# Two-layer conformer and latent-attention trunk: one stop of TensorE per unit of gate weights, four heads at four stages

## What is computed

```python
proj   = rms(x) @ w_in[l]                 # convolution input, latents, and 4 x 512 gate columns
u      = silu(layer_norm(depthwise_conv31(a * sigmoid(gate)) + conv_b))
y_conv = u @ w_conv_out[l]                # 512 -> 1024
q, k   = rope(rms(...)), rope(rms(...))   # per head, 96 wide
p      = softmax(mask(q @ k.T * scale))   # blocks of 128 queries; block 0 sees 128 keys, block 1 all 256
o      = p @ v                            # per head, 64 wide
y_mla  = o @ w_mla_out[l]                 # 512 -> 1024
gates  = sigmoid(proj[..., o4:] + gate_bias)
x      = x + (gates[0] * y_conv + gates[1] * y_mla) @ w_out[l]
```

## Time and profile before

| | |
|---|---|
| median of 3 runs | 1056.39 us |
| the profiled execution | 1056.12 us |
| its span, first to last instruction | 1054.3 us |
| outside the span | 1.8 us |
| TensorE busy | 1047.7 us (99% of the span) |
| VectorE busy | 677.6 us (64%) |
| ScalarE busy | 578.2 us (55%) |
| granted TensorE clock | 1.00 on the mean |

### The profile page before, as it was taken

One profiled execution on the slowest core, in us unless ns is written; L12 is line 12 of the kernel. 1 busy time (PEld: TensorE's weight loads), 2 busy tenths in 40 slices (PEclk: granted clock), 3 DMA queues, 4 the chain that ended last, 5 costly groups with the idle time before them and its releaser, 6 DMA issues.

```text
span 1054.3 us, 13846 instructions
## 1 busy us (share of the span) xinstructions
PE 1047.7 (99%) x5057; PEld 875.6 (83%) x5057; DVE 677.6 (64%) x897; ACT 578.2 (55%) x778; POOL 245.6 (23%) x258
## 2 busy tenths in 40 slices
PE   9999999999999999999999999999999999999998
PEld 6888888998888888888888888889978888888887
DVE  6755654698976666555476555646999667656551
ACT  7654544576872665445276454536778537545440
POOL 2960000148850000000048400001588300000000
PEclk9999999999999999999999999999999999999999
DMA  9977666455655396676469767655366356885641
GB/s 285 309 242 220 186 206 197 136 184 175 204 168 162 104 324 182 208 229 198 130 181 288 213 213 222 185 172 167 129 207 224 115 160 182 272 234 180 208 140 40
DMA packets 176771, 205.14 MB, mean 195 GB/s; under 512 B 49328, under 2 KB 147920, under 8 KB 176720
## 3 DMA queue, kind: packets, MB, share of 16 engines
q1 hardware_dynamic: 175504, 202.35, 61.4%
q10 hardware_dynamic: 1216, 2.11, 1.0%
HBM read 192.90 MB, written 1.05 MB: 184 GB/s over the span
## 4 chain that ended last, share of the span: by engine, by line
PE 88%; DVE 7%; DMA 2%; ACT 1%; issue 1%; SPq 0%; POOL 0%; ACTq 0%; DVEq 0%
PE bank L618 27%; PE bank L616 27%; PE bank L617 27%; DVE wlo L1433 2%; DVE bank L1601 2%; DMA raw<-in_w_in 1%; PE bank L697 1%; PE bank L655 1%; PE bank L892 1%; DVE small L1660 1%; PE bank L870 1%; PE bank L861 1%; DMA x<-in_x 1%; ACT whi L1076 0%; PE bank L894 0%
## 5 line engine op out<-in xcount | busy, mean ns | idle before, releaser
L1433 DVE TENSOR_TENSOR wlo<-raw,whi 128x2048 fp32r<-128x2048 f32 (+2 forms) x152 | 347.3, 2289 | 88.2 <-ACT whi L1076 87.1
L616 PE MATMUL bank<-whi,hThi 128*128 128x512 f32 (+1 forms) x976 | 378.9, 388 | 0.0
L618 PE MATMUL bank<-whi,hTlo 128*128 128x512 f32 (+1 forms) x976 | 373.7, 383 | 0.0
L617 PE MATMUL bank<-wlo,hThi 128*128 128x512 f32 (+1 forms) x976 | 373.5, 383 | 0.0
L1076 ACT ACTIVATE whi<-raw 128x2048 fp32r<-128x2048 f32 (+2 forms) x176 | 335.3, 1910 | 27.7 <-DMA raw<-in_ffn_w_up 17.2
L618 PEld LDWEIGHTS bank<-whi,hTlo 128*128 128x128 f32 x976 | 183.2, 188 | 35.9
L616 PEld LDWEIGHTS bank<-whi,hThi 128*128 128x128 f32 x976 | 183.3, 188 | 35.2 <-issue 0.6
L617 PEld LDWEIGHTS bank<-wlo,hThi 128*128 128x128 f32 x976 | 183.4, 188 | 34.8
L1145 ACT ACTIVATE gates<-bank,small 128x256 f32<-128x256 f32 x88 | 41.8, 475 | 275.6 <-PE bank L618 275.0
L616 PE MATMUL bank<-whi,gThi 128*128 128x512 f32 (+1 forms) x416 | 162.4, 390 | 0.0
L618 PE MATMUL bank<-whi,gTlo 128*128 128x512 f32 (+1 forms) x416 | 161.2, 387 | 0.0
(11 more groups left out here) (162 smaller groups left out, 819.6 us busy)
## 6 DMA issues: line engine op xcount, KB each, us to landing
raw<-in_ffn_w_down SPq DMA_DIRECT2D x88, 512.0 KB, 4.2
raw<-in_ffn_w_gate SPq DMA_DIRECT2D x84, 512.0 KB, 4.5
raw<-in_ffn_w_up SPq DMA_DIRECT2D x84, 512.0 KB, 5.6
raw<-in_w_in SPq DMA_DIRECT2D x48, 512.0 KB, 4.9
raw<-in_w_out SPq DMA_DIRECT2D x16, 512.0 KB, 4.3
raw<-in_w_in SPq DMA_DIRECT2D x8, 544.0 KB, 4.5
raw<-in_w_mla_out SPq DMA_DIRECT2D x8, 512.0 KB, 4.0
raw<-in_w_conv_out SPq DMA_DIRECT2D x8, 512.0 KB, 4.8
```

Source lines behind the costliest of these rows:

```text
L616: nc.tensor.matmul(out, lh, rh, start=start, stop=False, skip_group_check=skip)
L617: nc.tensor.matmul(out, lh, rl, start=False, stop=False, skip_group_check=skip)
L618: return nc.tensor.matmul(out, ll, rh, start=False, stop=stop, skip_group_check=skip)
L1433: nc.vector.tensor_tensor(wlo[:, slot(u0, RING), 0:n], raw[:, slot(u0, RAW), 0:n], whi[:, slot(u0, RING), 0:n].bitcast(F32), ALU.subtract) ...
```

## The change

The products of a gate unit stop once, at the unit's end, for four steps of four heads: `head_values(u8-2)`, `head_probs(u8-1)`, `head_scores(u8)`, `head_turn(u8+1)`. In the last unit `head_values(5)` stands ahead of t = 1 and `head_probs(6)` with `head_scores(7)` in the middle of t = 1, behind a wait for `ot_lo` of head 5. At the unit's end come `conv_turn`, `head_values(6)` and `head_probs(7)`; `head_values(7)` stands in the middle of the attention's output projection of t = 0, ahead of its unit i = 1, with waits for `ot_lo` of the heads 4 to 7. `head_probs` uses bank 6, `head_values` the last quarters of the banks 5 and 6, in three products of 128 columns with always 128 columns of stationary data, `conv_turn(1)` bank 4. The lists of ScalarE and VectorE are rewritten to match. On VectorE `head_rest(6)` and `head_rest(7)` both stand ahead of `bn_aggr`.

```diff
             def head_values(l, h):
                 pe.wait_ge(pt_ready, l * H + h + 1)
+                pe.wait_ge(max_ready, l * (2 * H) + min(2 * h + 4, 2 * H))
                 if h:
                     pe.wait_ge(ot_lo, l * H + h)
                 p = pT[:, h % 2, :]
-                n = (h % 2 + 1) * VD
-                v = vtok[:, :, h - h % 2:h + 1, :].rearrange("p t h d -> p t (h d)")
-                nc.tensor.matmul(bank[0:n, 6, 0:2 * P], v[:, 0, :], p[:, 0:2 * P], start=True, stop=False,
-                                 skip_group_check=True)
-                nc.tensor.matmul(bank[0:n, 6, P:2 * P], v[:, 1, :], p[:, 2 * P:3 * P], start=False, stop=True,
-                                 skip_group_check=True).then_inc(pv_done, 1)
+                v = vtok[:, :, h - h % 2:h - h % 2 + 2, :].rearrange("p t h d -> p t (h d)")
+                nc.tensor.matmul(bank[:, 5, 3 * P:4 * P], v[:, 0, :], p[:, 0:P], start=True, stop=True)
+                nc.tensor.matmul(bank[:, 6, 3 * P:4 * P], v[:, 0, :], p[:, P:2 * P], start=True, stop=False)
+                nc.tensor.matmul(bank[:, 6, 3 * P:4 * P], v[:, 1, :], p[:, 2 * P:3 * P], start=False,
+                                 stop=True).then_inc(pv_done, 1)
...
                     for t in range(TT):
-                        if u8 == 0 and t == 1:
+                        if (u8, t) == (0, 1):
                             head_turn(l, 0)
+                        if (u8, t) == (H - 1, 1):
+                            head_values(l, H - 3)
...
                         for k in range(4):
                             if (u8, t, k) == (H - 1, 1, 2):
-                                head_values(l, H - 2)
+
+                                pe.wait_ge(ot_lo, l * H + H - 2)
+                                head_probs(l, H - 2)
+                                head_scores(l, H - 1)
...
-                        if t == 0 and u8:
+                    if u8 < H - 1:
+
+                        if u8 > 1:
+                            head_values(l, u8 - 2)
+                        if u8:
                             head_probs(l, u8 - 1)
-                            head_scores(l, u8)
-                        if t == 1:
-                            if u8 == 0:
-                                head_scores(l, 0)
-                            elif u8 < H - 1:
-                                head_values(l, u8 - 1)
-
-                head_probs(l, H - 1)
+                        head_scores(l, u8)
+                        head_turn(l, u8 + 1)
+
                 for t in range(TT):
                     conv_turn(l, t)
-                head_values(l, H - 1)
-
-                def out_half(h):
-
-                    pe.wait_ge(ot_lo, l * H + 4 * h + 4)
+                head_values(l, H - 2)
+                head_probs(l, H - 1)
...
+                def last_values():
+
+                    head_values(l, H - 1)
+                    outputs(H - 2)
 
                 for t in range(TT):
                     pe.wait_ge(gate_sum, l * 8 + (6 if t == 0 else 8))
                     rows_out(l, UM + M_MLA, 2, gT, t, 2 - 2 * t, mla_done,
-                             between={0: lambda: out_half(0), 1: lambda: out_half(1)} if t == 0 else
+                             between={0: lambda: outputs(4), 2: last_values, 3: lambda: outputs(H)} if t == 0 else
                              {0: lambda: ln_turn(l)})
```

The list of VectorE (that of before is in the code above):

```diff
+                taps(8)
+                for h in range(H - 2):
+                    head_max(h)
+                    taps(3)
+                    head_sum(h)
+                    if h > 1:
+                        head_rest(h - 2)
+                    if h % 2:
+                        gate_bias(h // 2)
+                    taps(10)
+                head_max(H - 2)
+                taps(1)
+                head_rest(H - 4)
+                taps(2)
+                head_sum(H - 2)
+                taps(2)
+                head_rest(H - 3)
                 taps(4)
...
+                head_max(H - 1)
+                taps(3)
+                head_sum(H - 1)
                 taps(CT * W)
...
-                head_rest(H - 1)
+                for h in (H - 2, H - 1):
+                    head_rest(h)
                 for t in range(TT):
                     dve.wait_ge(ln_stats, l * TT + t + 1)
```

The list of ScalarE:

```diff
                 head_copy(0)
...
+                for h in range(H - 1):
+                    if h:
+                        head_probs(h - 1)
+                    head_copy(h + 1)
+                    if h == H - 2:
+
+                        act.wait_ge(max_ready, l * (2 * H) + 2 * h + 2)
+                        head_hi(h - 2)
+                        head_exp(h)
+                        head_scale(h)
+                        head_hi(h - 1)
                         one()
+                    else:
+                        head_exp(h)
+                        if h > 1:
+                            head_hi(h - 2)
+                        one()
+                        head_scale(h)
+                    if h % 2:
+                        gate_tanh(h // 2)
+                    elif h in (2, 4):
+                        one()
+                head_probs(H - 2)
+                head_exp(H - 1)
+                head_scale(H - 1)
                 head_probs(H - 1)
+                head_hi(H - 2)
                 head_hi(H - 1)
                 gate_tanh(3)
```

More of the change, by code:

```diff
@@ L905, in rows_out @@
                     for k in range(2):
+                        if 2 * i + k in between:
+                            between[2 * i + k]()
                         for m in range(2):
@@ L1045, in mixer @@
                 rows_out(l, UM + M_CO, 2, hT, 0, 4, co_done,
-                         between={0: lambda: conv_half(0), 1: lambda: conv_half(1)})
-                rows_out(l, UM + M_CO, 2, hT, 1, 6, co_done, between={1: lambda: y_turn(0)})
+                         between={0: lambda: conv_half(0), 2: lambda: conv_half(1)})
+                rows_out(l, UM + M_CO, 2, hT, 1, 6, co_done, between={2: lambda: y_turn(0)})
                 pe.wait_ge(yt_lo, l * 4 + 2)
-                rows_out(l, UM + M_WO, 4, hT, 0, 4, acc_done, between={3: lambda: y_turn(1)})
+                rows_out(l, UM + M_WO, 4, hT, 0, 4, acc_done, between={6: lambda: y_turn(1)})
                 pe.wait_ge(yt_lo, l * 4 + 4)
-                rows_out(l, UM + M_WO, 4, hT, 1, 2, acc_done, between={3: lambda: norm(l, 2, 0)})
+                rows_out(l, UM + M_WO, 4, hT, 1, 2, acc_done, between={6: lambda: norm(l, 2, 0)})
             pe.sem_inc(unit_free, RING)
@@ L1338, in head_hi @@
                     rows = slice(h % 2 * VD, (h % 2 + 1) * VD)
-                    nc.scalar.activation(gThi[rows, h // 2, :], bank[rows, 6, 0:SEQ], ACT.Copy).then_inc(ot_hi, 1)
+                    nc.scalar.activation(gThi[rows, h // 2, :].rearrange("p (t n) -> p t n", t=TT),
+                                         bank[rows, 5:7, 3 * P:4 * P], ACT.Copy).then_inc(ot_hi, 1)
                 def gate_tanh(g):
@@ L1354, in mixer @@
                 head_copy(0)
-                for u8 in range(1, 8):
-                    if u8 == 1:
-                        head_exp(0)
-                        head_scale(0)
-                    head_copy(u8)
-                    if u8 > 1:
-                        head_hi(u8 - 2)
-                    one()
-                    head_probs(u8 - 1)
-                    if u8 % 2 == 0:
-                        gate_tanh(u8 // 2 - 1)
-                    head_exp(u8)
-                    if u8 in (3, 5):
-                        one()
-                    if u8 == H - 1:
-                        head_hi(u8 - 1)
-                    head_scale(u8)
+                for h in range(H - 1):
[8 more added lines that the diff above has]
+                        head_hi(h - 1)
+                        one()
+                    else:
[11 more added lines that the diff above has]
+                head_scale(H - 1)
                 head_probs(H - 1)
+                head_hi(H - 2)
                 head_hi(H - 1)
@@ L1701, in head_rest @@
                     rows = slice(h % 2 * VD, (h % 2 + 1) * VD)
-                    rest(gTlo[rows, h // 2, :], bank[rows, 6, 0:SEQ], gThi[rows, h // 2, :]).then_inc(ot_lo, 1)
+                    rest(gTlo[rows, h // 2, :].rearrange("p (t n) -> p t n", t=TT), bank[rows, 5:7, 3 * P:4 * P],
+                         gThi[rows, h // 2, :].rearrange("p (t n) -> p t n", t=TT)).then_inc(ot_lo, 1)
                 def gate_bias(g):
@@ L1712, in gate_bias @@
                                                 bias[:, :], ALU.add).then_inc(gate_sum, 1)
-                taps(4)
-                head_max(0)
-                taps(2)
-                head_sum(0)
-                for u8 in range(1, 8):
-                    taps(4)
-                    if u8 > 1:
-                        head_rest(u8 - 2)
-                    taps(3)
-                    if u8 % 2 == 0:
-                        gate_bias(u8 // 2 - 1)
-                    head_max(u8)
```

(11 more changed lines are left out.)

21 lines of the change are left out of this document (9 added, 12 removed).

## The result

The changed kernel takes 1063.00 us (median of 6 runs, 1062.61 to 1064.74), the one before 1056.09 (6 runs, 1055.77 to 1056.65). The ratio is 1.0066, 95% interval 1.0055 to 1.0077: slower by 6.9 us. The forecast was 1060.6, with a range of 1057.4 to 1063.5.

The account below looks back on a forecast made before the run. TensorE, busy 1047.7 of 1054.3 us, was taken as the bound. Per layer -0.70 - 1.12 - 0.20 + 2.5 + 1.6 = +2.1 us, +4.2 for two layers: 1056.39 + 4.2 = 1060.6 us, range 1057.4 to 1063.5.

Parts of the forecast that it names:

- wait of `head_probs(0)`: Gate phase: TensorE's wait for head 0's scaled probabilities becomes hidden behind 24 products, -0.70 us a layer.
- narrow `head_values`: Even heads' 64-column operation becomes 128 columns, saving 0.28 us at each of four heads, -1.12 us a layer.
- five stops: Gate phase and projection: 12 stops instead of 17, at 0.04 us each, -0.20 us a layer.
- stall before `conv_turn`: First tail, end of the last unit: TensorE waits for VectorE's last taps, +2.5 us a layer (2.3 to 2.9).
- stall before `ln_turn`: Second tail, in the output projection: TensorE waits for the layer norm, +1.6 us a layer (1.4 to 1.9).
- clock: Rival: TensorE's clock falls to 1.2 GHz behind the stalls, adding 8.2 us, 1068.8; chance 0.05.
- The forecast's own bounds: Whole kernel: the terms' extremes give +1.6 to +3.1 us a layer, 1059.6 to 1062.6.
- The prediction's bound of 2.9: Upper end of the stall before `conv_turn`, if ScalarE's rounding ahead of `head_probs(6)` pushes `head_exp(7)`.
- The tails are hidden: Rival: VectorE's taps and layer norm keep ahead of TensorE, only -2.0 us a layer stands, 1052.4; chance 0.07.
- only the first tail is real: Rival: values to layer norm take under 2.8 us instead of 4.4, +0.5 a layer, 1057.4; chance 0.10.
- VectorE paces the middle: Rival: TensorE waits for probabilities up to 0.5 us in three units a layer, +3, 1063.5; chance 0.10.
- first rival: Tails hidden, kernel faster: decides when both stalls together stay under 1.5 us a layer; 1052.4, chance 0.07.

Follow-up runs that it names:

- experiment 4: Changed kernel with `head_rest(7)` behind `gate_bias(3)` instead of ahead of `bn_aggr`: 1059.24 us, ratio 1.0023.
- experiment 5: Changed kernel with four taps moved earlier into VectorE's idle time, none left behind `head_sum(7)`: 1058.36 us, ratio 1.0019.
- experiment 3: Kernel before with `head_probs(0)` six products later and, on ScalarE, `head_copy(1)` ahead of `head_exp(0)` and `head_scale(0)`: 1054.62 us, ratio 0.9986.
- experiment 1: Kernel before with `head_values` always on 128 columns of stationary data: 1054.11 us, ratio 0.9979.
- experiment 6: Changed kernel with ten bf16 matmuls of zeros put into the stall before `conv_turn`: 1061.62 us, ratio 1.0050.
- experiment 2: Kernel before with only `head_probs(0)` moved six products later, to a stop of its own: 1056.25 us, ratio 0.9999.
- experiments 8 and 9: Kernel before, two stops a unit kept: 8 with the edits of experiment 1 and experiment 2, 1055.27 us; 9 with those of experiment 1 and experiment 3, 1053.97 us.
- experiment 7: Changed kernel with the four taps ahead of `head_max(7)` moved behind it, lengthening the stall before `conv_turn`: 1068.29 us, ratio 1.0111.
- experiment 11: Changed kernel with both tails mended (1052.51 us) given a second stop again in units 2 to 6, for `head_values(u8-2)`: 1054.26 us.

## Why the prediction was right, and where it was short

**The sign and the place** were right. Both stalls are where the lists of the engines put them, and the experiments 4 and 5 took the second away (1.68 us a layer) and the first by as much as four taps are long (1.61 us a layer), as expected.

**Term by term, per layer.**

| term | predicted | measured |
|---|---|---|
| wait of `head_probs(0)` | -0.70 | -0.71 (experiment 3) |
| narrow `head_values` | -1.12 | -1.02 (experiment 1) |
| five stops | -0.20 | -0.10, an estimate at 0.02 each (units of 7.57 against 7.55) |
| stall before `conv_turn` | +2.5 | +2.76 |
| stall before `ln_turn` | +1.6 | +1.65 |
| sum | +2.1 | +2.55 (layer 0), +2.52 (both layers of experiment 6) |
| clock | 0 | +1.6 in layer 1 |

The measured terms sum to +2.58. For two layers +5.1 came from the stalls and gains where +4.2 was forecast, +1.6 from the clock, and +0.3 lies ahead of the changed stretch, within the spread of that part.

**The range** held by luck. The forecast's own bounds, +1.6 to +3.1 a layer, gave 1059.6 to 1062.6, or 3.2 to 6.2 us over the kernel before; measured were 1063.0 and 6.9. The stated range reached to 1063.5 only because it was widened for another rival, VectorE as the pace of the middle, which did not happen. What filled that room was the clock, for which the sum had nothing.

**The first stall** was 0.26 longer. The prediction let head 7's maximum start 0.05 behind the scores. VectorE's timeline of the changed kernel:

```profile
294.45 0.43 DVE L1454 TENSOR_TENSOR gTlo<-bank,gThi 64x256 fp32r<-64x256 f32 x1 [0.50 <-ACT gThi L1345]
294.91 1.67 DVE L1617 SCALAR_TENSOR_TENSOR bank<-cu,vec,bank 128x256 f32<-128x256 f32 x4
296.62 0.35 DVE L1704 CUSTOM_DVE_ANT_0 htok<-bank,mask,small 128x128 f32<-128x128 f32 x1
...
298.47 0.16 DVE L1713 RECIPROCAL small<-small 128x2 f32<-128x2 f32 x1
298.55 0.86 DVE L1617 SCALAR_TENSOR_TENSOR bank<-cu,vec,bank 128x256 f32<-128x256 f32 x2
299.31 0.88 DVE L1609 TENSOR_SCALAR cacc<-bank,vec 128x256 f32<-128x256 f32 x2
```

The scores' record ends at 296.26, the maximum starts at 296.62: VectorE had waited 0.50 for head 5's high part and had four taps to do first. From the maximum on the chain has the length predicted (3.57 us to the last tap). The prediction's bound of 2.9 allowed for this size, but for a delay on ScalarE. The term was mis-sized by the state of the engine that starts it.

**The wait that went** was rightly sized and wrongly explained. The prediction named the scaled probabilities, by the earlier trace rows, the row of the weight load. They were ready at 247.91, in time; late was ScalarE's copy of head 1 (experiment 2). The sum came out by luck: the change moves that copy ahead as well as the probabilities back.

**The narrow operation and the stop.** The 0.28 was 0.255 and the 0.04 was 0.02. The title of the change, one stop of TensorE a unit, is the smallest of its terms: 0.1 us a layer.

**The step that failed is the clock.** It stood as a rival with 0.05, on the ground that the clock had been 1.00 through the phase. That trace had no idle time over 0.5 us there, and so it said nothing about a stall of 2.8. The mechanism of this rival was right, its chance was too small and its price too high. It took as much loss as the stalls are long, 8.2 us; measured is about one fall in an execution, in which 3.4 us at half the clock (824.9 to 828.3) lose about half of that, 1.6 us. It made up most of the distance from 1060.6 to 1063.0. The Trainium skill ("TensorE: Matmul & The Clock Gate", section "HAM oscillation — how this bites in real kernels") says that gaps between bursts of matmuls can put the clock back. The runs here agree, with one fall behind two stalls of 2.8 us.

**The other rivals.** "The tails are hidden" and "only the first tail is real" are refuted by the list of waits. "VectorE paces the middle" didn't happen in the changed kernel, where units stay at 7.55; by their rows it is what took part of the gains in the experiments 8 and 9, whose list has 14 taps a unit where the changed one has 13.

**A slip in the first rival.** Its bound for the stalls, 2.0 less the half of 2.1 us, is 0.95 us a layer and not 1.5. Nothing hangs on it, as the stalls are 4.4.

## What to carry to other kernels

Where TensorE is the bound, ask first what each step waits for at its new place and which list, in order, produces it: here the saving of the stops was 0.1 us a layer, and the work that the regrouping put close before its consumers cost 4.4. Filler work that a later step waits for as a whole (the taps) belongs into the filler engine's idle time at the beginning, not behind its last urgent step. And where an instruction waits for several things, compare the end of each producer with the time at which the engine came: one row of the list named a producer that was done, and behind the first step stood a second one that needed the same late copy, so that moving one alone brought nothing.

## What the runs showed of the hardware

- TensorE's clock fell behind stalls of some 2.8 us, but not each time. The changed kernel has a mean granted clock of 0.998 in five of six runs and 0.997 in the sixth, which is the slowest (1064.74). An estimate from these means is one fall an execution in five and two in the sixth. In experiment 4, with one such stall a layer, seven of 11 runs have a mean granted clock of 0.998 and take 1058.69 to 1059.98 us; four have 1.000 and take 1057.19 to 1058.52. The medians of the two groups are 1.6 us apart (1059.41 and 1057.78), the same as the difference between the layers of one execution. With stalls of 1.1 and 1.65 us a layer (experiment 5) it never fell, granted clock 0.999 or more in 11 runs; behind 4.1 us it fell in both layers of the profile (experiment 7). Ten bf16 matmuls of zeros, 2.33 us in the stall, kept it up in five of five runs (experiment 6). The experiments 4 and 5 ran on one chip, 6 and 7 on another one, so neither contrast is one between chips.
- An operation with 64 columns of stationary data between ones with 128 or 96 cost 0.255 us at each place, at equal columns of moving data (experiment 1). Its weight load did not run under the product before it (idle 0.35 us), and the next one, of 96 columns, had 0.17 us of idle time. The Trainium skill ("TensorEngine Tiling (Array Packing)", section "Key Properties") says that changing the tiling mode drains the engine. The idle times fit that; that the 64-column operation changes the mode, no row shows. The turns between 96 and 128 in the other steps show no cost: a whole stop with them is 0.02 to 0.05.
- A stop is cheap when the weight load of its first step runs under the last product (0.02 to 0.05 us). Where that step's semaphore came only as the product ended, the load started behind it, and the unit was 0.16 to 0.30 us longer (experiment 11).
- What stays open: why the clock fell in layer 1 of the changed kernel and in layer 0 of experiment 4, behind stalls of the same length.
